# A routing stretch in which GpSimd and VectorE exchange two pieces of work

## The reference

```python
def peer_ffn(x, norm_ffn, w_query, sub_keys, expert_down, expert_up):
    xn = rmsnorm(x, norm_ffn)
    ...
        s = jnp.einsum('bthpd,hpnd->bthpn', q, sub_keys)
        s1, i1 = lax.top_k(s[..., 0, :], PEER_TOPK)
        s2, i2 = lax.top_k(s[..., 1, :], PEER_TOPK)
        ...
        idx = (jnp.take_along_axis(i1, top_c // PEER_TOPK, axis=-1) * PEER_N_KEYS
               + jnp.take_along_axis(i2, top_c % PEER_TOPK, axis=-1))
        g = jax.nn.softmax(top_s.astype(jnp.float32), axis=-1)
        u = jnp.take(expert_down, idx, axis=0)
        act = jax.nn.gelu(jnp.einsum('btd,bthkd->bthk', xi, u).astype(jnp.float32))
        v_sel = jnp.take(expert_up, idx, axis=0)
        return jnp.einsum('bthk,bthkd->btd', (g * act).astype(xi.dtype), v_sel)
```

## Time and profile before

| what | value |
|---|---|
| median of 3 runs | 3136.68 us |
| profiled execution: its own time, its span | 3137.76 us, 3135.9 us |
| busy, share of the span: TensorE, VectorE, ScalarE, GpSimd | 97%, 70%, 50%, 13% |
| TensorE's granted clock, mean | 0.98 of 2.4 GHz |
| first compare (L1966) of layer 0, of them all | 373.9 us, 128 in both layers |
| last compare of layer 0 | 604.4 us |
| a load of down rows, issue to landing | 3.6 us |

### The profile page before, as it was taken

How to read it: one execution, slowest core, us unless ns; L and a number is a source line. 1 busy time by engine, 2 the same in 40 slices (tenths; PEclk the granted TensorE clock), 3 DMA queues, 4 the chain that set the end, 5 groups by cost and what they waited for, 6 DMA issues and landing times. The chain is left out here.

```text
span 3135.9 us, 66433 instructions
## 1 busy us (share of the span) xinstructions
PE 3043.5 (97%) x25756; PEld 2955.6 (94%) x25756; DVE 2203.9 (70%) x3620; ACT 1578.3 (50%) x2760; POOL 417.1 (13%) x319
## 2 busy tenths in 40 slices
PE   9899999999999899999999999999999899999998
PEld 9799988999998799988999999999997799999898
DVE  4669799989996659799978887333255555554654
ACT  5464566655555664566655555232245344444443
POOL 0126322200001016422200000000020000000100
PEclk9999999999999999999999999999999899999899
DMA  6256544578896256644489995323342245555464
GB/s 186 91 162 195 182 144 144 170 261 287 288 363 210 84 160 193 192 142 146 147 270 314 318 313 193 100 94 97 98 113 77 79 137 187 168 192 177 137 193 146
DMA packets 172779, 560.64 MB, mean 179 GB/s; under 512 B 22480, under 2 KB 31440, under 8 KB 172000
## 3 DMA queue, kind: packets, MB, share of 16 engines
q1 hardware_dynamic: 172640, 558.83, 54.8%
HBM read 557.71 MB, written 1.05 MB: 178 GB/s over the span
## 5 line engine op out<-in xcount | busy, mean ns | idle before, releaser
L241 DVE TENSOR_TENSOR peer_e_lo<-raw,peer_e_hi 128x1024 fp32r<-128x1024 f32 x498 | 664.9, 1335 | 127.9 <-ACT peer_e_hi L237 123.7
L237 ACT ACTIVATE peer_e_hi<-raw 128x1024 fp32r<-128x1024 f32 x560 | 588.6, 1051 | 219.6 <-PE peer_e_out L1531 162.3
L241 DVE TENSOR_TENSOR ffn_lo<-raw,ffn_hi 128x1024 fp32r<-128x1024 f32 x256 | 312.9, 1225 | 464.2 <-ACT ffn_hi L237 464.2
L237 ACT ACTIVATE ffn_hi<-raw 128x1024 fp32r<-128x1024 f32 x264 | 279.2, 1061 | 527.0 <-PE ffn_acc L2811 333.1
L1527 PE MATMUL peer_e_out<-x_normed,peer_e_hi 128*128 128x256 f32 x2048 | 493.4, 283 | 3.6 <-ACT peer_e_hi L237 3.4
L1528 PE MATMUL peer_e_out<-x_normed,peer_e_hi 128*128 128x256 f32 x2048 | 481.2, 277 | 0.0
L1594 PE MATMUL peer_e_out<-peer_h_pair,peer_e_hi 128*128 128x256 f32 x2048 | 477.7, 276 | 0.4 <-DVE peer_e_lo L241 0.4
L1595 PE MATMUL peer_e_out<-peer_h_pair,peer_e_hi 128*128 128x256 f32 x2048 | 477.7, 276 | 0.0
L1527 PEld LDWEIGHTS peer_e_out<-x_normed,peer_e_hi 128*128 128x128 f32 x2048 | 385.2, 188 | 8.7 <-issue 8.7
L1528 PEld LDWEIGHTS peer_e_out<-x_normed,peer_e_hi 128*128 128x128 f32 x2048 | 385.4, 188 | 0.0
L1594 PEld LDWEIGHTS peer_e_out<-peer_h_pair,peer_e_hi 128*128 128x128 f32 x2048 | 384.5, 188 | 0.7 <-issue 0.7
(11 more groups left out here) (640 smaller groups left out, 6153.7 us busy)
## 6 DMA issues: line engine op xcount, KB each, us to landing
raw<-in_l_down SPq DMA_DIRECT2D x256, 512.0 KB, 3.6
raw<-in_l_up SPq DMA_DIRECT2D x256, 512.0 KB, 4.8
raw<-in_ffn_wi SPq DMA_DIRECT2D x176, 512.0 KB, 3.7
peer_e_ring<-in_w_mod SPq DMA_DIRECT2D x144, 512.0 KB, 5.2
raw<-in_ffn_wo SPq DMA_DIRECT2D x88, 512.0 KB, 3.6
raw<-in_l_peer_w_query SPq DMA_DIRECT2D x32, 512.0 KB, 3.6
raw<-in_w_in SPq DMA_DIRECT2D x26, 512.0 KB, 3.7
l_in_raw<-in_l_w_in SPq DMA_DIRECT2D x24, 512.0 KB, 4.4
```

What stands on the lines that cost most here:

```text
L237: return act.activation(hi, v, ACT.Copy)
L241: return eng.tensor_tensor(lo, v, hi.bitcast(F32), ALU.subtract)
```

## The change

In the units from 60 on GpSimd makes the low parts of the down rows (L241) instead of VectorE, and TensorE and SP count GpSimd's semaphore (`lo_pool`) there. The product with the low weights leaves GpSimd. VectorE does it itself in `make_hots`: the compare stays one instruction of 1024 elements, VectorE waits for its own compare (`plain`), and four tensor_scalar instructions of 128x128 f16 follow, one a token, each with a column of the low weights. ScalarE's weigh_hot waits for the last of them (`hot`).

```diff
@@ wait_lo_down
-            if n >= NS:
+            if n >= ROUTE_AT:
+                eng.wait_ge(lo_pool, NS - BY_VECTOR + n - ROUTE_AT + 1)
+            elif n >= NS:
                 eng.wait_ge(lo_vector, PRE + BY_VECTOR + n - NS + 1)
@@ TensorE
+            def score_pool(n, k):
+                score(n, k, lo_pool, n + (NS - BY_VECTOR - ROUTE_AT + 1), used, n - (RAWS - 1 + DIRECT))
...
-                    score_vector(i * RING + (k + ROUTE_AT), k, used, DIRECT)
+                    score_pool(i * RING + (k + ROUTE_AT), k)
                     route(i * RING + k, k)
@@ ScalarE, weigh_hot
-                act.wait_ge(hot_low, b + 1)
+                act.wait_ge(hot, b + 1)
@@ GpSimd
-            for b in range(BATCHES):
-                pool.wait_ge(hot, b + 1)
-                pool.tensor_tensor(hots[b % RING][:, 2], hots[b % RING][:, 1],
-                                   w_low[:, b * TOKS:(b + 1) * TOKS].unsqueeze(2).to_broadcast([P, TOKS, P]),
-                                   ALU.mult).then_inc(hot_low, 1)
+            for n in range(ROUTE_AT, NK):
+                low_down(n // RAWS, n % RAWS)
@@ VectorE, make_hots
-                dve.tensor_tensor(hots[b % RING][:, 0:2], iota_half.unsqueeze(1).unsqueeze(1).to_broadcast(both),
+                tile, tokens = hots[b % RING], range(b * TOKS, (b + 1) * TOKS)
+                dve.tensor_tensor(tile[:, 0:2], iota_half.unsqueeze(1).unsqueeze(1).to_broadcast(both),
                                   choice[:, 0:2, b * TOKS:(b + 1) * TOKS].unsqueeze(3).to_broadcast(both),
-                                  ALU.is_equal).then_inc(hot, 1)
+                                  ALU.is_equal).then_inc(plain, 1)
+                dve.wait_ge(plain, b + 1)
+                for a, t in enumerate(tokens):
+                    ins = dve.tensor_scalar(tile[:, 2, a], tile[:, 1, a], w_low[:, t:t + 1], None, ALU.mult)
+                ins.then_inc(hot, 1)
@@ VectorE, the units
-                if n > NS:
+                if NS < n < ROUTE_AT:
                     low_down(n)
```

More of the change, by code:

```diff
@@ L1269, in peer_experts @@
             st.sem(x) for x in ("v_step", "shifted", "exped", "chosen", "turned", "copied"))
-        hot, hot_low, hot_w, routed, weighted = (
-            st.sem(x) for x in ("hot", "hot_low", "hot_w", "routed", "weighted"))
+        plain, hot, hot_w, routed, weighted = (
+            st.sem(x) for x in ("plain", "hot", "hot_w", "routed", "weighted"))
         hi_up, lo_up, hi_h, lo_h, out_sum = (
@@ L1582, in _ @@
             for k in range(RING):
-                score_vector(ROUTE_AT + k, k, used, DIRECT)
+                score_pool(ROUTE_AT + k, k)
                 route(k, k, k < G_RING)
@@ L1586, in _ @@
                 for k in range(RING):
-                    score_vector(i * RING + (k + ROUTE_AT), k, used, DIRECT)
+                    score_pool(i * RING + (k + ROUTE_AT), k)
                     route(i * RING + k, k)
             for n in range(ROUTE_END, NK):
-                score_vector(n, n % RAWS, used, DIRECT)
+                score_pool(n, n % RAWS)
             def high(c, k, first=False):
@@ L1962, in make_hots @@
             def make_hots(b):
-                both = [P, 2, TOKS, P]
                 if b >= RING:
                     dve.wait_ge(routed, b - RING + 1)
-                dve.tensor_tensor(hots[b % RING][:, 0:2], iota_half.unsqueeze(1).unsqueeze(1).to_broadcast(both),
+                tile, tokens = hots[b % RING], range(b * TOKS, (b + 1) * TOKS)
+                both = [P, 2, TOKS, P]
+                dve.tensor_tensor(tile[:, 0:2], iota_half.unsqueeze(1).unsqueeze(1).to_broadcast(both),
                                   choice[:, 0:2, b * TOKS:(b + 1) * TOKS].unsqueeze(3).to_broadcast(both),
-                                  ALU.is_equal).then_inc(hot, 1)
+                                  ALU.is_equal).then_inc(plain, 1)
[3 more added lines that the diff above has]
+                ins.then_inc(hot, 1)
             def weigh(b, units):
```

## The result

The changed kernel took 3340.05 us (median of four runs, 3329.3 to 3348.6), the kernel before 3139.74 in the same comparison. The ratio is 1.0635, 95% interval 1.0593 to 1.0677: 6.3% slower, about 200 us. The direction was forecast, the size was not: 3254 was forecast, with a range up to 3325. The profiled execution took 3329.34, its span 3327.3, 191.4 more than the span before.

What follows compares the result with a forecast made beforehand. VectorE was taken to bound a routing unit of 128 experts at 3.66 us. Exclusion with GpSimd would make it 4.6: 124 x 0.94 = 117 us on 3137.8, less 1.1 for the median, so 3254 us, range 3172 to 3325.

Steps and rivals of the forecast that it cites:

- the new exclusive work (4.0): Per routing unit, GpSimd's low part 2.40, compare behind it 1.08, 0.05 and rows 0.5 run one after the other: 4.0 us.
- rival 2: Rival in the experiments, called late: GpSimd's 2.4 us low parts reach TensorE too late; no chance given.
- step (4): Loop through ScalarE's weighing: GpSimd asks 2.37 to 2.49 us after zero, inside VectorE's rows, the fourth row at 2.53.
- zero: The moment of VectorE's last row instruction of the unit before, from which the prediction counts its times.
- the choice of 4.6: Middle taken between units of 4.3 and 4.9 us, 0.94 more than 3.66; forecast case (4.2 to 4.9) had chance 0.72.
- Rhythm A: GpSimd gets in before VectorE's fourth row in every unit; weighing and use never lie beside it: 4.9 us a unit.
- step (2): VectorE gains four 128-element row instructions a unit, starts 0.14 us apart; its own work becomes about 2.7 us.
- the race: Whether GpSimd gets in before VectorE's fourth row (4.9 us a unit) or after (4.3): 0.1 us that no row decides.
- Long rows: Rival: VectorE's rows take 0.28 us each, every one split by GpSimd's place; unit 5.2, 3328 us; chance 0.10.
- No lock: Rival: compare or rows don't exclude GpSimd's low part; TensorE's 3.40 us decides the unit, 3105 us; chance 0.06.
- the sentence on four elements a cycle: 16-bit tensor_scalar from SBUF at that rate puts the fourth row early, favouring 4.3 us a unit: 79 us more, about 3216.
- At 24 us: Trace of the kernel before: GpSimd gets in between VectorE instructions, and the VectorE one takes 0.97 us instead of 0.47.

Runs made afterwards that it cites:

- e2: Changed kernel without the four row instructions, product with the low weights left out, TensorE's second route product taking the high one again: 3100.91 us, ratio 0.9856 to the kernel before.
- e4: Kernel before with VectorE making the row instructions and keeping the low parts, GpSimd's loop in the stretch gone: 3174.97 us, ratio 1.0102.
- e1: Changed kernel with one wait added: GpSimd starts its low part only after VectorE's last row instruction of the unit: 3228.02 us, ratio 1.0259 to the kernel before.
- e5: Changed kernel with the use moved from behind the weighing to between compare and row instructions: 3291.89 us, ratio 1.0474 to the kernel before.
- e6: Kernel before without GpSimd's product with the low weights, TensorE's second route product taking the high one again: 3094.31 us, ratio 0.9847.
- e8: Kernel before with GpSimd's product cut to two of four tokens, ScalarE making the other two: 3091.12 us, ratio 0.9814.
- e7: Kernel before with VectorE's unit reordered to low part, compare, weighing, use: 3100.19 us, ratio 0.9884.
- e9: Changed kernel with GpSimd's low part from unit 60 on replaced by a memset of the same tile: 3122.71 us, one run.
- e3: Changed kernel with the four row instructions made one tensor_tensor of 128x512: 3249.13 us, ratio 1.0336 to the kernel before.

## Why the prediction was wrong

**What held.** The mechanism and its place: VectorE and GpSimd exclude each other, the new exclusive work (4.0) is more than the old unit (3.66), one row instruction is held up in nearly every unit (2.42 instead of 0.25), and TensorE waits for the weighing. e2 and e4 each take one party away and the loss is gone or is 1%; e1 keeps all the work and moves one start, for 112 us; e2 and TensorE's 0.7 us of waiting for the low part leave nothing for rival 2. GpSimd's request was worked out as 2.37 to 2.49 after the last row of the unit before, and comes at 2.46 (452.31 less 449.85, which is 455.06 less a unit). The granted clock was 0.980 in the mean before and 0.975 after. It did fall in places of the stretch: 1.00 before, 0.96 now in the window above, 0.91 in the 40 us from 520 on, 0.83 from 560 to 580, and 1.00 again behind, so part of that time was at 1.2 GHz. In the 20 us before it fell TensorE was busy for 13.0, at 1.00. It cost the unit nothing: from 560 to 580 TensorE was busy for 16.9 us where it was 13.8 in the 20 us behind, which came out of its gaps, and the compares stayed 5.20 to 5.22 apart.

**What failed: step (4), the times of VectorE from zero, and through them the choice of 4.6.** Rhythm A was the right one, but it was sized 4.9, and it is 5.2. Two terms were short. The use was given 0.60 behind the weighing's start. That 0.60 was read where another instruction follows the weighing. In the changed order the use follows it, and waits for it by a semaphore: 0.78 (454.98 to 455.76), 0.18 more. And rows start 0.17 apart, not the 0.14 of step (2). So the rows start 2.3 after zero instead of 2.11, the second is due at 2.47, and GpSimd at 2.46 gets in before it, not before the fourth. After it three rows are left instead of one, 0.32 more. The unit is 2.46 + 2.37 + 0.38 = 5.21. e5 shows it: with the wait hidden the rows start 1.99 after zero, GpSimd gets in before the fourth and the unit is 4.90. VectorE's own work was short for the same reasons: the terms of step (2) add up to 2.79, not 2.7, and without the blocked part of the compare e1 has 3.04.

**And the value taken, 4.6.** Between 4.3 and 4.9 the middle was taken because the race could not be read. It was no race but a lock-step: once in between, GpSimd is in between in every unit, since its request hangs on the row that it delays; 57 of the 63 distances of layer 0 are 5.2 to 5.3, with a mean of 5.13 (323.0 over 63), and in 56 of its 64 batches it is the second row that is held up. Of the 0.6 that the unit came out too long, 0.3 is this and 0.3 the terms above; 0.6 x 124 = 74 us brings the forecast to 3328, the profiled execution's 3329. That it fits to 1 us is partly luck: the compares of the two layers account for 185 us, and what the other 6 outside them are is open. The median lies 11 higher; what makes executions of this kernel differ by 19 us is not settled (e1 has 21, the kernel before 35 over its runs on several chips).

**The rivals.** "Long rows" named the right unit, 5.2, by luck, for another reason: the rows are 0.25, close to its 0.28, but only one of them is held off. "No lock" priced TensorE's floor at 3.40 from one unit; e6 shows 3.25 and e8 3.23, so that rival was some 20 us too slow as well. The early fourth row that the sentence on four elements a cycle leads to did not come: 128 elements take 0.25 with starts 0.17 apart (e4); no run shows the rate itself. At 24 us the prediction sets 0.97 against 0.47, which is another form's time; the same form took 0.42 at 17.51. Nothing rests on the difference.

## What to carry to other kernels

Before work is swapped between GpSimd and VectorE, add up what must run one after the other on both, and compare that sum with the unit, not each engine's load: here both were under it. Then look at which VectorE instructions don't exclude GpSimd (here those with an input in PSUM), and time GpSimd's start so that it lies beside them; the order of four instructions was worth 1.2% (e7), and one wait more took the ratio from 1.0635 to 1.0259 (e1). A request that hangs on the instruction it delays repeats in every unit, so its place is to be worked out and not averaged. When an instruction gets a new neighbour, read its distance anew: a wait that another instruction used to cover comes with the move.

## What the runs showed of the hardware

A VectorE tensor_scalar of 128x128 f16 with a column operand took 0.25 us alone (e4) and up to 2.48 beside a GpSimd subtraction; it was held off by a memset too, which a compare with two SBUF inputs was not (e9). A GpSimd instruction that is ready gets in between two VectorE instructions whose starts are 0.17 us apart, and is itself held off where VectorE's instruction runs already (2.79 and 3.10 instead of 2.38 in e3). A GpSimd product of 128x256 f16 took 0.61 us, of 128x512 1.04.
